# Three edits to the start of the mixture-of-experts stages of a fused transformer kernel: where expert 2's weights are asked for, where the first tokens are gathered, and 24 transposes of the identity on TensorE

## The chip, the cores and the metric

The kernel is one program on one core of a Trainium2 chip. Its time is that of one execution on the device, in microseconds (us). The engines named below are TensorE (PE, with its weight loads as PEld), VectorE (DVE), ScalarE (ACT), GpSimd (POOL) and SyncE (SP). SP does no arithmetic here, it issues the large DMA transfers. POOL issues the indirect ones, which gather or scatter rows by an index.

## The reference

Two blocks run one after the other on 512 tokens of width 1024 in float32. The first has two layers with a mixture of experts each; the second is a hybrid attention layer with a dense MLP. The change lies in the two mixtures, 768 tokens in layer 0 (512 and 256 context tokens) and 512 in layer 1:

```
lg = t @ wr_g + br_g ; g = argmax(lg)                       # 4 groups
le = (t @ wr_e + br_e) of group g                           # 8 experts in a group
top_v, top_i = top_k(le, 2)
weights = softmax(lg)[g] * softmax(top_v)
for each of the 32 experts, over the tokens that chose it:
    hidden = silu(x @ w_gate[e]) * (x @ w_up[e])            # 1024 -> 512
    y = hidden @ w_down[e]                                  # 512 -> 1024
out[token] += weight * y
```

The weights of one expert are three matrices of 1024 x 512 float32, 2 MB (2,097,152 bytes) each. All 32 experts are read in both layers, whatever the tokens chose.

## The kernel before

The program is a chain of phases. Each phase has its own tiles and semaphores and one block of code for each engine; between two phases all five engines meet at a barrier (line 127 in the profile), so a phase begins when the slowest engine has left the one before. The barrier is gathered by POOL. A layer's phases around the change are:

- `project_out` (out0, out1): the attention's output projection, residual, second norm and the router's logits, tile by tile of 128 tokens. SP asks for the projection's weights, the vectors, and then, in `load_expert(sp, e, ring, 0, 0)`, for all three matrices of expert 0. After that it stores each normalised tile `h` to DRAM (line 1160); `h` has two buffers, so the norm of tile i waits until the store of tile i-2 has landed (line 1291 is the instruction behind that wait).
- `route`: on DVE and PE, from the logits to a table `r["index"]` that lists, for each expert, 64 token slots. Each token row is two halves of 512 numbers, so a block of 64 tokens is a tile of 128 x 512. SP asks for experts 1 and 2, six transfers of 2 MB.
- `experts` (moe0, moe1): 32 blocks, one per expert. The weights lie in a ring of three slots; expert i lies in slot i % 3. SP's `refill` asks for the gate matrix of expert i+3 as soon as PE has done the gate products of expert i (semaphore `gated`), then for up (`upped`), then for down (`downed`). POOL gathers the tokens of block i+2 once PE has transposed those of block i, and scatters the results.

In block i PE does 32 gate products (line 1823; the profile counts each float32 matmul of this kind twice), 32 up products, the transposes of the tokens of block i+1 (line 1807), two transposes of the hidden values, and 16 down products (line 1869). Before block 0 it waits for `x_in[0]`, the first gather, and transposes it (`turn_x(0)`).

At the start of `experts` DVE clears the two token tiles `xg` and the last expert's tile (line 2055, `cleared`), since a slot without a token is not written by the gather. POOL copies one column of the index (line 1729), waits for `cleared` and issues the gather (line 1734); it does so for blocks 0 and 1, and then goes on as PE frees tiles. DVE then computes the tokens' weights and the count of extra blocks (for experts with over 64 tokens), which no engine needs in block 0.

The ring's slots are allotted from the right side of SBUF: slot 0 before `project_out`, the gate and up parts of slot 2 and all others after it (`add_first_slot`, `add_other_slots`).

## Time and profile before

| | |
|---|---|
| three runs | 2841.88, 2844.44, 2845.53 us; median 2844.44 |
| profiled execution | 2844.95 us, span 2843.1 us |
| PE busy | 2463.8 us (87%) |
| DVE, ACT, POOL busy | 1004.4, 552.0, 166.1 us |
| DMA | 599.29 MB moved; 425 GB/s in most slices of both expert stages |
| layer 0: first weight issue in routing, first refill | 658.33, 691.82 us |
| layer 1: first weight issue in routing, first refill | 1518.60, 1548.69 us |

The page divides the span of 2843.1 us into 40 slices of 71 us. Slices 11 to 16 and 22 to 28 move 415 to 426 GB/s: those are the two expert stages. A timeline row reads: start in us, duration of the merged piece, engine, line, operation, output<-input, count, and in brackets how long the engine had been idle and what ended that. Windows rows give, for a stretch, the busy time of each engine with the number of its instructions, TensorE's granted clock as a share of full speed (1.00 is 2.4 GHz, 0.50 is 1.2 GHz), the busy share of the DMA engines, and the rate.

### The profile page before, as it was taken

What the parts mean: (1) busy time and instruction counts of PE and PEld (TensorE: products, weight loads), DVE (VectorE), ACT (ScalarE), POOL (GpSimd) and SP (SyncE); (2) the same over time, 40 slices, a digit from 0 to 9 for tenths busy, and PEclk for the clock granted to TensorE, in tenths of its full rate; (3) what the DMA queues carried; (4) which work ended last, traced back from release to release, by engine and by line L of the source; (5) the groups of instructions that cost most, each with busy time, mean ns of one, the idle gap of its engine ahead of it and who ended that gap; (6) DMA issues with size and microseconds to landing.
All of it is one profiled execution on the core that took longest, in us unless ns stands there. A gap on an engine that the chain in (4) does not pass through costs nothing. (4 is left out here: it accounts for less than half of the span.)

```text
span 2843.1 us, 30780 instructions
## 1 busy us (share of the span) xinstructions
PE 2463.8 (87%) x12293; PEld 1297.5 (46%) x12293; DVE 1004.4 (35%) x2156; ACT 552.0 (19%) x1229; POOL 166.1 (6%) x270
## 2 busy tenths in 40 slices
PE   7999898795997777797986998788697789999999
PEld 4444366443553333344743553434343654444444
DVE  3211177665322222465734322222365452110000
ACT  3000077311000000114711100000122541000000
POOL 0000000001121111000001121111000000000000
PEclk9999899896999999898997999999898899999999
DMA  8555400507999999711056999999700140212110
GB/s 279 203 193 178 166 15 1 210 30 298 424 425 425 426 425 426 282 45 34 2 195 276 423 424 425 425 425 424 281 16 1 51 168 25 89 59 89 59 59 30
DMA packets 112474, 599.29 MB, mean 211 GB/s; under 512 B 22796, under 2 KB 33332, under 8 KB 82632
## 3 DMA queue, kind: packets, MB, share of 16 engines
q1 hardware_dynamic: 101768, 576.26, 50.6%
q0 software_dynamic: 10560, 21.01, 1.9%
q8 instruction: 101, 1.65, 0.2%
q14 instruction: 45, 0.37, 0.0%
HBM read 580.35 MB, written 30.49 MB: 215 GB/s over the span
## 5 line engine op out<-in xcount | busy, mean ns | idle before, releaser
L1823 PE MATMUL moe_gate<-moe_wg,moe_xg_t 128*64 128x256 f32 x1984 | 244.4, 398 | 50.1 <-DMA moe_wg<-in_moe_w_gate 48.6
L1869 PE MATMUL moe_down<-moe_wd,moe_hid_t 128*64 128x512 f32 x1024 | 235.5, 601 | 47.3 <-DMA moe_wd<-in_moe_w_down 34.1
L1823 PE MATMUL moe_up<-moe_wu,moe_xg_t 128*64 128x256 f32 x1984 | 239.3, 392 | 42.9 <-DMA moe_wu<-in_moe_w_up 42.9
L490 PE MATMUL qkv_acc<-qkv_w,a_buffer 128*128 128x512 f32 x512 | 225.7, 594 | 0.3 <-PE qkv_mod_acc L379 0.3
L3125 PE MATMUL mlp_acc<-m_h,mlp_w 128*128 128x512 f32 x512 | 223.3, 597 | 2.9 <-PE mlp_acc L3125 1.8
L1823 PEld LDWEIGHTS moe_gate<-moe_wg,moe_xg_t 128*64 128x64 f32 x1984 | 149.1, 138 | 162.7 <-DMA moe_wg<-in_moe_w_gate 82.0
L3142 PE MATMUL mlp_acc<-mlp_w,mlp_u_t 128*128 128x512 f32 x512 | 220.0, 592 | 0.3 <-PE mlp_acc L3125 0.3
L1823 PEld LDWEIGHTS moe_up<-moe_wu,moe_xg_t 128*64 128x64 f32 x1984 | 145.7, 135 | 132.3 <-DMA moe_wu<-in_moe_w_up 61.9
L3125 PEld LDWEIGHTS mlp_acc<-m_h,mlp_w 128*128 128x128 f32 x512 | 97.3, 191 | 128.5 <-issue 128.5
L3142 PEld LDWEIGHTS mlp_acc<-mlp_w,mlp_u_t 128*128 128x128 f32 x512 | 97.2, 190 | 123.1 <-issue 122.8
L2052 DVE COPY moe_y<-moe_down 128x512 f32<-128x512 f32 x62 | 42.9, 692 | 311.6 <-PE moe_down L1869 311.6
L1343 PE MATMUL out_acc<-out_w,out_o_t 128*128 128x512 f32 x320 | 149.9, 629 | 2.8 <-ACT out_o_t L1186 2.8
L1869 PEld LDWEIGHTS moe_down<-moe_wd,moe_hid_t 128*64 128x64 f32 x1024 | 73.5, 137 | 165.1 <-issue 123.7
L490 PEld LDWEIGHTS qkv_acc<-qkv_w,a_buffer 128*128 128x128 f32 x512 | 94.8, 190 | 113.9 <-issue 108.5
L1916 ACT ACTIVATE moe_sig<-moe_gate 128x256 f32<-128x256 f32 x64 | 24.6, 384 | 550.9 <-PE moe_gate L1823 550.9
L2039 DVE TENSOR_SCALAR moe_sig<-moe_sig 128x256 f32<-128x256 f32 x62 | 18.4, 297 | 271.7 <-ACT moe_sig L1916 271.7
L2041 DVE RECIPROCAL moe_sig<-moe_sig 128x256 f32<-128x256 f32 x62 | 108.7, 1753 | 2.1
L1758 POOL DMA_INDIRECT moe_results<-moe_y,moe_y_idx x62 | 64.3, 1038 | 712.3 <-DVE moe_y L2052 712.3
L1343 PEld LDWEIGHTS out_acc<-out_w,out_o_t 128*128 128x128 f32 x320 | 63.8, 202 | 82.3 <-issue 77.8
L1909 ACT COPY moe_xg_t<-moe_x_tp 128x512 f32<-128x512 f32 x64 | 37.5, 586 | 318.3 <-PE moe_x_tp L1807 318.3
L3162 DVE TENSOR_TENSOR mlp_u_t<-mlp_u_t 128x512 f32<-128x512 f32 x32 | 22.2, 692 | 207.4 <-ACT mlp_u_t L3156 207.4
L745 PE MATMUL dif_score<-a_k,a_q 64*128 64x256 f32 (+1 forms) x320 | 65.9, 525 | 23.5 <-ACT dif_prob L849 19.9
(441 smaller groups left out, 3015.8 us busy)
## 6 DMA issues: line engine op xcount, KB each, us to landing
moe_wg<-in_moe_w_gate SPq DMA_DIRECT2D x64, 2048.0 KB, 42.6
moe_wu<-in_moe_w_up SPq DMA_DIRECT2D x64, 2048.0 KB, 42.6
moe_wd<-in_moe_w_down SPq DMA_DIRECT2D x64, 2048.0 KB, 42.7
qkv_mod_w<-in_mod_w SPq DMA_DIRECT2D x42, 1024.0 KB, 4.9
mlp_w<-in_w_up SPq DMA_DIRECT2D x8, 2048.0 KB, 12.7
mlp_w<-in_w_down SPq DMA_DIRECT2D x8, 2048.0 KB, 7.9
qkv_w<-in_a_w_qkv SPq DMA_DIRECT2D x12, 1024.0 KB, 9.6
moe_results<-dif_zeros SPq DMA_DIRECT2D x12, 512.0 KB, 5.2
```

Source lines behind the costliest of these rows:

```text
L490: mm = nc.tensor.matmul(acc[i % 4][:], h_t[:, k, t * P:(t + 1) * P], w[:, c % w_ring, k, :], start=(k == 0), stop=(k == KD - 1))
L745: mm = nc.tensor.matmul(unit(g, m)[:, n0:n0 + w], q_t[rows, h, t * P:(t + 1) * P], k_t[rows, h, n0:n0 + w], start=True, stop=True)
L1343: mm = nc.tensor.matmul(acc[j % 3][:], lhs(k), w[:, c, k, :], start=(k == 0), stop=(k == KD - 1))
L1758: nc.gpsimd.indirect_dma_start(result_halves, bass.IndirectOffsetOnAxis(ap=y_idx[b][:], axis=0), y[b][:], None, bounds_check=last_result, ...
L1823: mm = nc.tensor.matmul(acc[b][halves[f], 0:HF], x_t[:, k, c, :], w[:, c, k, :].rearrange("p (q f j) -> p f q j", f=2, j=2)[:, f], start=( ...
L1869: mm = nc.tensor.matmul(down[b][halves[c], :], hid_t[:, k, h, :], wd[z][:, 2 * h + k, c * NCHUNK:(c + 1) * NCHUNK], start=(k, h) == (0, 0) ...
L1909: nc.scalar.copy(xg_t[b][:].rearrange("p k c n -> p k (c n)"), x_tp[:]).then_inc(s["read_x"], 1)
L1916: nc.scalar.activation(sig[:], gate[b][:, 0:HF], ACT.Exp, scale=-1.0).then_inc(s["expd"], 1)
L2041: nc.vector.reciprocal(sig[:], sig[:]).then_inc(s["step"], 1)
L2052: nc.vector.tensor_copy(y[b][:], down[b][:]).then_inc(s["y_done"], 1)
L3125: mm = nc.tensor.matmul(acc[i % 8][:], wj[:, k, q * P:(q + 1) * P], h_t[:, k, :], start=(k == 0), stop=(k == KD - 1))
L3142: mm = nc.tensor.matmul(acc[2 * t + c][:], u_t[:, f, t * P:(t + 1) * P], wj[:, q, c * NCHUNK:(c + 1) * NCHUNK], start=(f == 0), stop=(f == ...
```

## The change

- `project_out` asks for the gate and up matrices of expert 2 right behind expert 0's, if slot 2 already has its tiles. That is so in layer 1 alone, where the new `add_second_slot` allots them before the phase. Layer 0 asks as before.
- `route` then asks, in layer 1, for expert 1 and the down matrix of expert 2: four transfers of 2 MB, not six.
- `route` has a part for POOL: it clears the three token tiles (DVE's clearing in `experts` is gone), waits for the index (`indexed`), copies its first two columns and issues the gathers of blocks 0 and 1. The token tiles, their index tiles and the semaphores `x_in` move from the `experts` phase into the ring's record. This is so in both layers.
- In `experts`, PE does 24 transposes of the identity into an accumulator that nothing reads before block 1 overwrites it, ahead of its wait for the first gather. This is so in both layers.

```diff
@@ project_out, SP @@
             if ring is not None:
                 load_expert(sp, e, ring, 0, 0)
+                if 2 in ring["wg"]:
+                    load_gate(sp, e, ring["layer"], ring, 2, 2)
+                    load_up(sp, e, ring["layer"], ring, 2, 2)
@@ route @@
         def _(sp):
-            for b in range(1, RING):
-                load_expert(sp, e, ring, b, b)
+            load_expert(sp, e, ring, 1, 1)
+            if second_begun:
+                load_down(sp, e, layer, ring, 2, 2)
+            else:
+                load_expert(sp, e, ring, 2, 2)
+
+        @block.gpsimd
+        def _(pool):
+            for x in (*ring["xg"], ring["y"]):
+                nc.gpsimd.memset(x[:], 0.0).then_inc(s["cleared"], 1)
+            pool.wait_ge(s["indexed"], 1)
+            for b in range(2):
+                nc.gpsimd.tensor_copy(ring["x_idx"][b][:], r["index"][:, 0, b:b + 1]).then_inc(
+                    s["idx_done"], 1)
+            pool.wait_ge(s["cleared"], 3)
+            for b in range(2):
+                gather_tokens(nc, e, ring, b, lambda: pool.wait_ge(s["idx_done"], 2))
...
-            v.tensor_scalar(r["index"][:, :, 0:NE], slots[:], half[:], None, ALU.add)
+            v.tensor_scalar(r["index"][:, :, 0:NE], slots[:], half[:], None, ALU.add).then_inc(
+                s["indexed"], 1)
@@ the ring @@
+WARM = 24
+def add_second_slot(nc, ring):
+    for name in ("wg", "wu"):
+        add_part(nc, ring, "second", name, 2)
+def gather_tokens(nc, e, ring, b, idx_done):
+    rows = e["h_dram"].rearrange("r (h d) -> (r h) d", h=2)
+    idx_done()
+    nc.gpsimd.indirect_dma_start(
+        ring["xg"][b][:], None, rows, bass.IndirectOffsetOnAxis(ap=ring["x_idx"][b][:], axis=0),
+        bounds_check=rows.shape[0] - 1, oob_is_err=False).then_inc(ring["x_in"][b], 16)
@@ experts, POOL, PE and DVE @@
-            for b in range(2):
-                gather(b, b, b + 1)
...
+            for _ in range(WARM):
+                nc.tensor.transpose(down[1][:, 0:P], e["ident"][:], e["ident"][:])
             pe.wait_ge(x_in[0], 16)
             turn_x(0)
...
-            for x in (*xg, xg_l):
-                v.memset(x[:], 0.0).then_inc(s["cleared"], 1)
             token_weights()
@@ layer_1 @@
         add_first_slot(nc, ring)
+        add_second_slot(nc, ring)
...
-        route(nc, e, 1, stream, logits, r, ring)
+        route(nc, e, 1, stream, logits, r, ring, True)
```

How the instructions stand. On SP, in layer 1 from the projection's end into routing, before:

```order
L1572 DMA moe_wg<-in_moe_w_gate 128x4096
L1579 DMA moe_wu<-in_moe_w_up 128x4096
L1586 DMA moe_wd<-in_moe_w_down 128x4096
L1160 DMA moe_tokens<-out_h 128x1024 x4
L127 UNCONDITIONAL_BRANCH
L1410 UNCONDITIONAL_BRANCH
L1572 DMA moe_wg<-in_moe_w_gate 128x4096
L1579 DMA moe_wu<-in_moe_w_up 128x4096
L1586 DMA moe_wd<-in_moe_w_down 128x4096
L1572 DMA moe_wg<-in_moe_w_gate 128x4096
L1579 DMA moe_wu<-in_moe_w_up 128x4096
L1586 DMA moe_wd<-in_moe_w_down 128x4096
```

and after:

```order
L1610 DMA moe_wg<-in_moe_w_gate 128x4096
L1617 DMA moe_wu<-in_moe_w_up 128x4096
L1624 DMA moe_wd<-in_moe_w_down 128x4096
L1610 DMA moe_wg<-in_moe_w_gate 128x4096
L1617 DMA moe_wu<-in_moe_w_up 128x4096
L1163 DMA moe_tokens<-out_h 128x1024 x4
L127 UNCONDITIONAL_BRANCH
L1414 UNCONDITIONAL_BRANCH
L1610 DMA moe_wg<-in_moe_w_gate 128x4096
L1617 DMA moe_wu<-in_moe_w_up 128x4096
L1624 DMA moe_wd<-in_moe_w_down 128x4096 x2
```

The gate and up transfers of expert 2 now stand ahead of the four stores of `h`, and four weight transfers are left behind them.

On POOL, around the start of layer 0's experts, before (`route0_...` and `moe0_...` are semaphores of those phases, `barrier_...gather` is the barrier between two phases):

```order
L127 UNCONDITIONAL_BRANCH
L132 ISA [waits barrier_Pool_Activation_PE_DVE_SP_gather] x3
L1722 UNCONDITIONAL_BRANCH
L1729 COPY moe_x_idx<-r_index 128x1
L1734 DMA moe_xg<-moe_tokens,moe_x_idx 128x512 [waits moe0_idx_done,moe0_cleared]
L1729 COPY moe_x_idx<-r_index 128x1
L1734 DMA moe_xg<-moe_tokens,moe_x_idx 128x512 [waits moe0_idx_done,moe0_cleared]
L1729 COPY moe_x_idx<-r_index 128x1 [waits moe0_turned_x]
```

and after:

```order
L132 ISA [waits barrier_Pool_Activation_PE_DVE_SP_gather] x2
L1422 UNCONDITIONAL_BRANCH
L1425 MEMSET moe_xg 128x512 x2
L1425 MEMSET moe_last_y 128x512
L1428 COPY moe_x_idx<-r_index 128x1 [waits route0_indexed]
L1428 COPY moe_x_idx<-r_index 128x1
L1586 DMA moe_xg<-moe_tokens,moe_x_idx 128x512 [waits route0_idx_done,route0_cleared]
L1586 DMA moe_xg<-moe_tokens,moe_x_idx 128x512 [waits route0_idx_done]
L127 UNCONDITIONAL_BRANCH
L132 ISA [waits barrier_Pool_Activation_PE_DVE_SP_gather]
L1758 UNCONDITIONAL_BRANCH
L1765 COPY moe_x_idx<-r_index 128x1 [waits moe0_turned_x]
```

The clearing, two index copies and two gathers now stand ahead of the barrier that ends routing; behind it POOL begins with the gather for block 2.

On PE, from the last routing products of layer 0 into block 0, before:

```order
L1429 MATMUL route_slots<-route_what,route_lane 64x64 [waits route0_lane_done]
L1429 MATMUL route_slots<-route_what,route_lane 64x64 x11
L127 UNCONDITIONAL_BRANCH
L1802 UNCONDITIONAL_BRANCH [waits barrier_Pool_Activation_PE_DVE_SP_release]
L1807 MATMUL moe_x_tp<-ident_sb,moe_xg 128x128 [waits moe0_x_in0]
L1807 MATMUL moe_x_tp<-ident_sb,moe_xg 128x128 x3
L1823 MATMUL moe_gate<-moe_wg,moe_xg_t 64x256 [waits moe0_read_x,moe0_g_in0]
L1823 MATMUL moe_gate<-moe_wg,moe_xg_t 64x256 x15
L1823 MATMUL moe_up<-moe_wu,moe_xg_t 64x256 [waits moe0_u_in0]
L1823 MATMUL moe_up<-moe_wu,moe_xg_t 64x256 x15
```

and after:

```order
L1448 MATMUL route_slots<-route_what,route_lane 64x64 x11
L127 UNCONDITIONAL_BRANCH
L1834 UNCONDITIONAL_BRANCH [waits barrier_Pool_Activation_PE_DVE_SP_release]
L1907 MATMUL moe_down<-ident_sb 128x128 x24
L1839 MATMUL moe_x_tp<-ident_sb,moe_xg 128x128 [waits moe0_x_in0]
L1839 MATMUL moe_x_tp<-ident_sb,moe_xg 128x128 x3
L1855 MATMUL moe_gate<-moe_wg,moe_xg_t 64x256 [waits moe0_read_x,moe0_g_in0]
L1855 MATMUL moe_gate<-moe_wg,moe_xg_t 64x256 x15
L1855 MATMUL moe_up<-moe_wu,moe_xg_t 64x256 [waits moe0_u_in0]
```

Between the barrier's release and the wait for the first gather (`moe0_x_in0`) there are 24 transposes of the identity.

## Rows read from the trace of the kernel before

**Rows 1.** The page's list of DMA issues: count, size of each, us to landing.

```profile
moe_wg<-in_moe_w_gate SPq DMA_DIRECT2D x64, 2048.0 KB, 42.6
```

**Rows 2.** Windows, middle of layer 1's expert stage: busy us by engine, clock, DMA share, GB/s.

```profile
1700.00:1720.00 20.00, 16.29 (x118) 8.28 (x118) 3.69 (x6) 1.65 (x4) 4.95 (x8) 1.00 1.01 426
```

**Rows 3.** PE in order of time, ends of both expert stages: start, us, [idle before <-releaser].

```profile
1144.53 3.65 PE L1869 MATMUL moe_down<-moe_wd,moe_hid_t 128*64 128x512 f32 x16 [0.59 <-DMA moe_wd<-in_moe_w_down]
...
1990.35 3.65 PE L1869 MATMUL moe_down<-moe_wd,moe_hid_t 128*64 128x512 f32 x16 [0.63 <-DMA moe_wd<-in_moe_w_down]
1996.80 5.45 PE L1823 MATMUL moe_gate<-moe_wg,moe_xg_t_l 128*64 128x256 f32 x32 [2.80 <-DMA moe_wg<-in_moe_w_gate]
```

**Rows 4.** SP's DMA issues in order of time, routing of layer 1 and after.

```profile
1518.60 0.33 SPq L1572 DMA_DIRECT2D moe_wg<-in_moe_w_gate  x1
...
1521.24 0.45 SPq L1586 DMA_DIRECT2D moe_wd<-in_moe_w_down  x1
1548.69 0.33 SPq L1572 DMA_DIRECT2D moe_wg<-in_moe_w_gate  x1
```

**Rows 5.** Windows, layer 1, from the first issue of the routing stage to the first refill.

```profile
1518.60:1525.00 6.40, 0.72 (x2) 0.50 (x2) 5.49 (x25) 1.28 (x1) 0.00 (x0) 0.50 0.86 317
1525.00:1548.50 23.50, 10.16 (x73) 6.79 (x74) 9.24 (x42) 0.90 (x3) 5.11 (x9) 0.52 1.01 427
```

**Rows 6.** PE in order of time, first block of layer 1.

```profile
1540.61 1.11 PE L1807 MATMUL moe_x_tp<-ident_sb,moe_xg 128*128 128x128 f32 x4 [11.05 <-DMA moe_xg<-moe_tokens,moe_x_idx]
1542.49 6.17 PE L1823 MATMUL moe_gate<-moe_wg,moe_xg_t 128*64 128x256 f32 x32 [0.77 <-ACT moe_xg_t L1909]
1548.48 3.80 PE L1823 MATMUL moe_up<-moe_wu,moe_xg_t 128*64 128x256 f32 x32
```

**Rows 7.** DVE and POOL in order of time, between routing and experts, layer 1.

```profile
1529.60 0.28 DVE L1487 TENSOR_SCALAR r_index<-route_slots,half_sb 128x64 int32<-128x64 f32 x1 [1.56 <-PE route_slots L1429]
...
1530.40 0.19 POOL L1729 COPY moe_x_idx<-r_index 128x1 int32<-128x1 int32 x1 [356.10 <-POOLq L127]
1532.49 1.06 POOL L1734 DMA_INDIRECT moe_xg<-moe_tokens,moe_x_idx  x1 [1.91 <-DVE moe_last_y L2055]
...
1534.61 1.04 POOL L1734 DMA_INDIRECT moe_xg<-moe_tokens,moe_x_idx  x1 [0.85 <-POOL moe_x_idx L1729]
```

**Rows 8.** Windows, layer 0, around the first refill.

```profile
690.00:695.00 5.00, 5.00 (x43) 3.30 (x42) 2.47 (x3) 0.38 (x1) 0.00 (x0) 0.93 0.74 241
```

**Rows 9.** POOL, PE and SP in order of time, same stretch of layer 0.

```profile
674.81 1.20 POOL L1734 DMA_INDIRECT moe_xg<-moe_tokens,moe_x_idx  x1 [1.65 <-DVE moe_last_y L2055]
...
683.62 1.12 PE L1807 MATMUL moe_x_tp<-ident_sb,moe_xg 128*128 128x128 f32 x4 [11.49 <-DMA moe_xg<-moe_tokens,moe_x_idx]
685.50 6.29 PE L1823 MATMUL moe_gate<-moe_wg,moe_xg_t 128*64 128x256 f32 x32 [0.77 <-ACT moe_xg_t L1909]
...
691.82 0.33 SPq L1572 DMA_DIRECT2D moe_wg<-in_moe_w_gate  x1
```

**Rows 10.** Windows in the first gate products of layer 1.

```profile
1547.50:1548.00 0.50, 0.50 (x6) 0.30 (x4) 0.00 (x0) 0.00 (x0) 0.00 (x0) 1.00 0.84 356
```

**Rows 11.** PE in order of time, transposes of the second block's attention.

```profile
2202.03 5.42 PE L2882 MATMUL turn_tp<-ident_sb,c_hh 128*128 128x128 f32 x32 [2.64 <-DVE turn_dk L2849]
```

**Rows 12.** Windows in those transposes.

```profile
2203.00:2206.00 3.00, 3.00 (x16) 2.79 (x15) 1.53 (x5) 2.06 (x5) 0.00 (x0) 0.50 0.37 62
2207.00:2208.00 1.00, 1.00 (x12) 1.00 (x10) 0.96 (x2) 1.00 (x3) 0.00 (x0) 1.00 0.07 16
```

**Rows 13.** POOL in order of time, the clearing of a tile of zeros.

```profile
340.37 0.95 POOL L733 MEMSET dif_zeros<- 128x1024 f32 x1 [338.69 <-POOLq L127]
```

**Rows 14.** SP and DVE in order of time, layer 1's output projection.

```profile
1465.45 0.33 SPq L1160 DMA_DIRECT2D moe_tokens<-out_h  x1
...
1490.53 2.00 DVE L1291 SCALAR_TENSOR_TENSOR out_h<-res,out_n_rstd,out_mul 128x1024 f32<-128x1024 f32 x1 [0.31 <-DVE out_n_rstd L162]
```

**Rows 15.** Windows, layer 1's output projection.

```profile
1465.00:1470.00 5.00, 3.70 (x25) 3.32 (x26) 3.71 (x6) 2.13 (x3) 0.00 (x0) 0.90 0.58 243
```

More of the change, by code:

```diff
@@ L1384, in max_extra, with route @@
     return 4 * nt
-def route(nc, e, layer, tiles, logits, r, ring):
+def route(nc, e, layer, tiles, logits, r, ring, second_begun):
     nt = len(tiles)
@@ L1405, in route @@
         where, slots = ph.ps("where", [P, nt + 1, NE]), ph.ps("slots", [P, 2, NE])
-        names = "zeroed hot_done what_done where_done lane_done slots_done gexp_in wexp_in step"
+        names = ("zeroed hot_done what_done where_done lane_done slots_done gexp_in wexp_in cleared indexed "
+                 "idx_done step")
         s = {x: ph.sem(x) for x in names.split()}
@@ L1499, in weight_ring @@
                 next_in=[one(f"next_in{c}") for c in range(5)], vec_in=[one(f"vec_in{x}") for x in range(2)],
-                last_out=one("last_out"))
+                last_out=one("last_out"), x_in=[one(f"x_in{b}") for b in range(2)])
 def add_part(nc, ring, scope, name, b):
@@ L1512, in add_first_slot @@
         add_part(nc, ring, "first", name, 0)
+def add_second_slot(nc, ring):
+    for name in ("wg", "wu"):
+        add_part(nc, ring, "second", name, 2)
 def add_other_slots(nc, ring):
-    add_part(nc, ring, "second", "wg", 2)
-    add_part(nc, ring, "second", "wu", 2)
+    if 2 not in ring["wg"]:
+        add_second_slot(nc, ring)
     for name, shape, dt in (("y", [P, NCHUNK], F32), ("hit", [P, P], F32), ("share", [P, 1], F32),
@@ L1525, in add_other_slots @@
         add_part(nc, ring, "scope", name, 1)
+    for name, shape, dt in (("xg", [P, D // 2], F32), ("x_idx", [P, 1], I32)):
+        ring[name] = [ring["scope"].enter_context(
+            nc.sbuf_tensor(f"moe{ring['layer']}_{name}{b}", shape, dt, side="right")) for b in range(2)]
 def flat(part):
@@ L1644, in experts @@
         wg, wu, wd = ring["wg"], ring["wu"], ring["wd"]
-        xg = [ph.sb(f"xg{b}", [P, D // 2]) for b in range(2)]
+        xg, x_idx, x_in = ring["xg"], ring["x_idx"], ring["x_in"]
         xg_t = [ph.sb(f"xg_t{b}", [P, 4, 2, TB]) for b in range(2)]
-        x_idx = [ph.sb(f"x_idx{b}", [P, 1], I32) for b in range(2)]
         y_idx = [ph.sb(f"y_idx{b}", [P, 1], I32) for b in range(2)]
@@ L1677, in experts @@
         part = [gate[0][:], up[0][:]]
-        names = ("y_free cleared idx_done turned_x read_x gated upped expd hid_done indexed landed "
+        names = ("y_free idx_done turned_x read_x gated upped expd hid_done indexed landed "
                  "turned_h read_h downed y_done step x_step x_tables_done x_slots_done x_read x_ready "
@@ L1681, in experts @@
         s = {x: ph.sem(x) for x in names.split()}
-        x_in = [nc.alloc_semaphore(f"moe{layer}_x_in{b}") for b in range(2)]
         x_in_l = nc.alloc_semaphore(f"moe{layer}_x_in_l")
@@ L1731, in gather @@
                 pool.wait_ge(s["idx_done"], count)
-                pool.wait_ge(s["cleared"], 2)
                 pool.sem_inc(s["indexed"], 1)
@@ L1743, in gather_last @@
                 pool.wait_ge(s["idx_l_done"], 1)
-                pool.wait_ge(s["cleared"], 3)
                 pool.sem_inc(s["indexed"], 1)
@@ L1769, in _ @@
                     pool.wait_ge(s["x_ready"], 1)
-                gather(b, i + 2 if i + 2 < last else i + 3, 2 * i + 3)
+                gather(b, i + 2 if i + 2 < last else i + 3, 2 * i + 1)
                 if i == 0:
                     gather_last()
-                scatter(b, i, i, 2 * i + 4)
+                scatter(b, i, i, 2 * i + 2)
                 if i >= 1:
@@ L1783, in two_extra @@
                     pool.wait_ge(s["turned_x"], i + 1)
-                    gather(b, i + 3, 2 * i + 3)
-                    scatter(b, i + 1, i, 2 * i + 4)
+                    gather(b, i + 3, 2 * i + 1)
+                    scatter(b, i + 1, i, 2 * i + 2)
                     pool.wait_ge(y_out[1 - b], 16 * (NE // 2 + i2))
@@ L2139, in layer_0 @@
     with ring["scope"]:
-        route(nc, e, 0, tiles, logits, r, ring)
+        route(nc, e, 0, tiles, logits, r, ring, False)
         experts(nc, e, 0, tiles, r, ring, TC, enter_1_loads)
@@ L2380, in layer_1 @@
         add_first_slot(nc, ring)
+        add_second_slot(nc, ring)
         project_out(nc, e, "out1", o, stream, None, None, 1.0, e["b_w_o"][0], mod_part(e, 1, 2),
```

## The prediction

> **What bounds the kernel now.** I read the page's slices first: both expert stages move some 425 GB/s from end to end. Then the windows of one of them: PE is busy 16.3 of 20 us at full clock while the DMA engines are busy all the time, at 426 GB/s [rows 2]. Then PE's order of time where each stage ends: the last full block's down products still wait for their weights [rows 3]. So each stage is one stream of 2 MB transfers (2.097 MB each [rows 1], 4.93 us at 425 GB/s), and PE follows it. The layer ends when the stream ends plus a fixed tail: an instant by which the whole stream comes earlier is an instant off the total, and an engine made faster in mid-stream is worth nothing.
>
> Next, where the stream has a hole. Its head start in routing is six transfers. The seventh is asked for when PE has done the first gate products: at 1548.69 in layer 1 [rows 4], right after those products (1542.49 + 6.17 = 1548.66 [rows 6]). In layer 1 the rate up to then is 427 GB/s [rows 5]: no hole. In layer 0 the same request, at 691.82 [rows 9], comes late, and the window around it shows 241 GB/s [rows 8]: (1 - 241/425) x 5 = 2.2 us of stream lost. A stream that starts from nothing loses too: from the first issue at 1518.60 to 1525 it made 317 GB/s [rows 5], (1 - 317/425) x 6.4 = 1.6 us, which I take as the price of a start.
>
> **Part 1, expert 2's gate and up in layer 1's projection.** Two transfers leave the routing stream: 2 x 4.93 = 9.9 us. But four transfers and the first two gathers (128 x 512 float32, 0.26 MB each) are 8.91 MB, 21.0 us, so the stream runs dry at 1518.6 + 1.6 + 21.0 = 1541.2, before the first refill can be asked for. So the gain is decided by when PE finishes gate products 0, that is by parts 2 and 3.
>
> What the two transfers cost where they now stand: the queue goes quiet at about 1465 + 5 x 243/425 = 1467.9 [rows 15]; 9.9 us more makes it 1477.7, while the projection's matmuls have their weights already. The first store of h is issued at 1465.45, and the norm that needs its buffer again starts at 1490.53 [rows 14]. Cover 12.8 us, cost nothing; if the cover is gone, each us late is a us lost (last rival).
>
> **Part 2, the gathers.** The index is ready at 1529.60 + 0.28 = 1529.88 [rows 7]. Before, POOL passed the barrier, copied at 1530.40 and then waited for DVE's clearing until 1532.49. Now: two copies of 0.2, 0.85 from a copy to the gather behind it, so the first gather at about 1531.2, 1.3 us sooner. Before it took 1540.61 - 1532.49 = 8.1 us until PE had the tokens [rows 6, 7], and the stream is as full in this stretch as before, so they land at 1539.3. The third gather and the last expert's come behind block 0's token transposes as before; POOL has nothing queued behind them that is urgent.
>
> What is added: the clearing is now on POOL, at the head of routing. 1024 columns took 0.95 us [rows 13], so three tiles of 512 cost 1.4 us, done 10 us before the index. It lies beside DVE's short routing operations. The trace has no POOL clearing beside busy DVE; bounds are 0 and, if the two engines exclude one another for all of it, 1.4 us. I take 0.4, near the lower end, since an engine writing its own tile is the nearest row. DVE loses its 1.5 us of clearing, which were on the path only through the gather. And the barrier: routing now ends for all engines only after POOL's second gather, at 1531.2 + 1.06 + 1.04 + 0.44 = 1533.7, not 1530.4. DVE's weights and counts begin 3.3 us later less 1.5; the first value that block 0 needs from DVE is behind the gate products, which ended at 1548.66 before [rows 6], so that is hidden.
>
> **Part 3, the 24 transposes.** They begin at 1533.7. Four transposes at half clock took 1.11 us [rows 6], so at most 24 x 0.28 = 6.7 us; 32 in a row, partly at full clock, took 5.42 [rows 11], so at least 24 x 0.17 = 4.1. Middle 5.4: they end at 1539.1, just before the tokens at 1539.3 (bounds 1537.8 and 1540.4). So T0, the start of token transposes, is 1539.4.
>
> What they are to give is the clock. Before, block 0's gate products ran at a mean of 0.52 [rows 5]; the clock rose to 1.00 at 1547.5 [rows 10], with PE at work since 1540.61. They took 6.17 us where the up products took 3.80 [rows 6]; the token transposes took 1.11, against 0.66 by the same ratio. In the attention of the second block PE did nothing but transposes from 2202.03 on [rows 11], at 0.50 at first and at 1.00 by 2207 [rows 12]. So transposes alone do raise the clock here. The Trainium skill says the opposite in "TensorE: Matmul & The Clock Gate", Part 4: a transpose does not count as PE activity and full clock "doesn't engage" for it. By that rule the 24 give nothing; by the row they give all. I follow the row, and the other way is a rival.
>
> At full clock the gate products end at T0 + 0.66 + 0.77 + 3.80 = T0 + 5.2 = 1544.6, or 1545.1 if the token transposes are still slow. I take 1544.9, 3.8 us sooner than before.
>
> **Sum.** Layer 1: the stream is dry from 1541.2 until 1544.9 + 1.6 = 1546.5, 5.3 us. In that hole the two next gathers move 0.52 MB, 1.2 us of what the stream would carry later. Gain 9.9 - 5.3 + 1.2 = 5.8. Layer 0: nothing leaves its stream, but the refill is asked for 3.8 us sooner, at 688.0; the stream ends at 691.82 + 1.6 - 2.2 = 691.2, later than 688.0 + 1.6, so the hole closes: gain 2.2, and 1.6 us in hand. Less 0.4 for the clearing: 7.6 us. From the profiled execution, 2844.95 (1.85 over its span, which stays), that is 2837.4. The median of the three runs stands 0.5 lower, which makes 2836.9; I say 2837.1.
>
> **The rivals.** A change of 0.2%, 5.7 us, is about what can be told from none.
>
> The clock does not rise (the page's rule, or the clock falls again while PE waits for the tokens). For it: the clock was at 0.50 through routing's small products. Against: rows 11 and 12. Gate products then end at T0 + 8.05 = 1547.5. Layer 1: 5.8 - 2.6 = 3.2. Layer 0: the request comes at 690.6, 1.0 past need, gain 1.2. Less 0.4: 4.0 us, 2841.0.
>
> The wait turned into another: barrier and transposes are later than the tokens. If the second gather needs the 0.85 pause too and each transpose takes 0.28, they run from 1534.5 to 1541.2, T0 1.8 later: layer 1 gives 4.0, layer 0 2.0, sum 5.6, 2839.3. For it: the barrier is gathered by POOL, the order shows the transposes ahead of the wait, and PE can't leave them. Against: it needs both upper ends.
>
> Better than forecast: the tokens land sooner, or the clock is up earlier than I put it, T0 + 5.2 with T0 at 1538. 1.7 us more, 2835.4. The gather's 8.1 us speaks against it.
>
> Slower: the stores of h behind the extra weights. At 1465.45 there are 1.04 + 4.19 = 5.2 MB ahead of the first store. Every us past 1490.5 stops the norm of tile 2, PE's transposes and the router behind it. The gain of 7.6 is eaten when the store lands at 1498.1, that is at 160 GB/s; over 0.2% slower needs 1503.8, 136 GB/s, and gives 2851. For it: the queue is one and in order. Against: the same stretch moved 243 GB/s in a window of which it was busy 0.58 [rows 15], so over 400 while busy.
>
> **How the numbers follow.** Forecast 0.60 (0.55 of it beyond 0.2%), better 0.08, no clock 0.13, later transposes 0.15 (half of it beyond 0.2%), slower 0.04. Faster 0.55 + 0.08 + 0.07 = 0.70, same 0.05 + 0.13 + 0.08 = 0.26, slower 0.04. The range takes in the better case with 0.8 us of spread below it, and above it the case without clock and the whole price of the clearing in layer 1: 2834.6 to 2842.0.
>
> **What would show it.** In the changed profile: five weight issues in the projection of layer 1 and the same norm start after the first store; a gather some 1.3 us after the index, in routing; PE's 24 transposes from 3.3 us after where it used to arrive, and a granted clock of 1.00 before the gate products, which take 3.8 us in both layers; first refill 3.8 us sooner against the first issue in both; in layer 0 no window under 415 GB/s around it, in layer 1 one with a hole of some 5 us before it; then blocks at the old pace to the end. The forecast is wrong if the clock is at 0.50 in the gate products, if the tokens or the transposes come later than 1540 by that clock, if routing's DVE chain is longer by over a us, or if the stream at 425 GB/s turns out not to carry its earlier start to the stage's end.

## The result

| | us |
|---|---|
| changed kernel, 22 runs | median 2852.19 (2847.47 to 2870.25) |
| kernel before, 22 runs beside them | median 2843.55 |
| ratio, 95% interval | 1.0027 [1.0015, 1.0039] |
| changed kernel, profiled execution | 2852.25, span 2850.4 |

The change makes the kernel 0.27% slower, 8.6 us by the medians. The forecast was 2837.1 (2834.6 to 2842.0), with a chance of 0.04 for slower: the measured time is 10.2 us above the range, and the sign is wrong. Two of the profiled executions read below, of the gathers alone (2860.20 us) and of 64 transposes alone (2854.86), are 11 to 12 us over their medians; the surplus lies behind layer 1's expert stage (860.3 and 861.5 us from there to the end, 849.1 before), so their stages can be read.

### The profile page after: what moved, and what is told of

It reads as the page before. It is cut to its first block and busy times, and to the rows that moved or that the text cites. A ratio compares the mean times of both kernels' runs of the same rounds, so it can differ in the third digit from the quotient of the medians.

```text
span 2850.4 us, 30876 instructions
## 1 busy us (share of the span) xinstructions
PE 2461.1 (86%) x12341; PEld 1301.5 (46%) x12341; DVE 1001.6 (35%) x2150; ACT 551.5 (19%) x1229; POOL 168.2 (6%) x276
```

## The profile after

I read it in the order of the prediction's steps. First POOL, in order of time, from the start of routing in layer 1; it answers to [rows 7] and [rows 13].

```profile
1521.73 0.98 POOL L1425 MEMSET moe_xg<- 128x512 f32 x2 [343.53 <-POOLq L127]
1522.66 0.53 POOL L1425 MEMSET moe_last_y<- 128x512 f32 x1
1533.24 0.30 POOL L1428 COPY moe_x_idx<-r_index 128x1 int32<-128x1 int32 x2 [10.06 <-DVE r_index L1506]
1534.43 1.07 POOL L1586 DMA_INDIRECT moe_xg<-moe_tokens,moe_x_idx  x1 [0.89 <-POOL moe_x_idx L1428]
1535.81 1.02 POOL L1586 DMA_INDIRECT moe_xg<-moe_tokens,moe_x_idx  x1 [0.31 <-issue]
```

POOL does what was forecast, when it was forecast: the first gather 1.26 us after the index (1532.89 + 0.28 = 1533.17), the second 1.38 behind the first, its last instruction of routing over at 1536.83. By the prediction's term the next phase should begin 0.44 us later, at 1537.3. PE and DVE in order of time, the same layer, against [rows 6]:

```profile
1545.50 5.35 PE L1907 MATMUL moe_down<-ident_sb 128*128 128x128 f32 x24 [12.65 <-PEq L127]
1550.65 0.85 PE L1839 MATMUL moe_x_tp<-ident_sb,moe_xg 128*128 128x128 f32 x4
1552.27 3.85 PE L1855 MATMUL moe_gate<-moe_wg,moe_xg_t 128*64 128x256 f32 x32 [0.77 <-ACT moe_xg_t L1943]
```

```profile
1532.89 0.28 DVE L1506 TENSOR_SCALAR r_index<-route_slots,half_sb 128x64 int32<-128x64 f32 x1 [1.56 <-PE route_slots L1448]
1545.50 0.17 DVE L1985 TENSOR_REDUCE moe_chosen<-r_tg 128x4 f32<-128x16 f32 x1 [12.32 <-PEq L127]
```

PE had been idle for 12.65 us and DVE for 12.32, both at line 127, the barrier. They leave it at 1545.50, 8.7 us after POOL's last instruction. What was in flight in those 8.7 us is in the list of DMA issues for the two gathers of routing (last number: median us from issue to landing):

```profile
moe_xg<-moe_tokens,moe_x_idx POOLq DMA_INDIRECT x2, 8.9
```

The 8.9 is the middle of the two: the first took 8.6 us, the second 9.3. So the second landed at 1535.81 + 9.3 = 1545.1, 0.4 us ahead of the barrier's end. In layer 0 it was issued at 676.12, took 10.5 us and landed at 686.6, again 0.4 us ahead of PE's first work at 687.01. The windows say the same from the DMA side, and stand against [rows 5] (us, busy by engine, clock, DMA share, GB/s):

```profile
1525.00:1540.00 15.00, 3.75 (x36) 2.82 (x36) 5.78 (x22) 0.31 (x2) 2.39 (x4) 0.50 1.02 434
1540.00:1543.00 3.00, 0.00 (x0) 0.00 (x0) 0.00 (x0) 0.00 (x0) 0.00 (x0) 0.50 0.95 399
1543.00:1544.50 1.50, 0.00 (x0) 0.00 (x0) 0.00 (x0) 0.00 (x0) 0.00 (x0) 0.50 0.17 60
1544.50:1545.50 1.00, 0.00 (x0) 0.03 (x1) 0.00 (x0) 0.00 (x0) 0.00 (x0) 0.50 0.00 0
...
1548.50:1550.00 1.50, 1.50 (x9) 1.50 (x8) 1.26 (x8) 0.00 (x0) 0.00 (x0) 0.50 0.00 0
1550.00:1552.00 2.00, 1.50 (x9) 1.26 (x7) 1.14 (x7) 0.47 (x1) 0.18 (x1) 0.71 0.00 0
1552.00:1556.00 4.00, 3.73 (x34) 2.81 (x36) 0.00 (x0) 0.12 (x1) 2.43 (x4) 1.00 0.08 22
```

The stream thins out at about 1543, hardly any bytes move after 1544.5, and only then does an engine move. Here the weights and the gathers end nearly together, so this trace alone does not say which of them the barrier waits for. The transposes then run with every DMA engine silent: they are on the path, all 5.2 us of them. They do what they were put there for, the clock is at 1.00 in the gate products, which take 3.85 us and not 6.17. The first refill answers to [rows 4]; above it the weight issues of routing:

```profile
1521.47 0.33 SPq L1610 DMA_DIRECT2D moe_wg<-in_moe_w_gate  x1
...
1522.33 1.24 SPq L1624 DMA_DIRECT2D moe_wd<-in_moe_w_down  x2
1556.14 0.33 SPq L1610 DMA_DIRECT2D moe_wg<-in_moe_w_gate  x1
```

Layer 0, PE and SP in order of time, against [rows 9]:

```profile
687.01 4.74 PE L1907 MATMUL moe_down<-ident_sb 128*128 128x128 f32 x24 [14.04 <-PEq L127]
691.59 0.60 PE L1839 MATMUL moe_x_tp<-ident_sb,moe_xg 128*128 128x128 f32 x4
692.96 3.84 PE L1855 MATMUL moe_gate<-moe_wg,moe_xg_t 128*64 128x256 f32 x32 [0.77 <-ACT moe_xg_t L1943]
...
696.83 0.33 SPq L1610 DMA_DIRECT2D moe_wg<-in_moe_w_gate  x1
```

When the index is ready varies by several us from one execution to the next, from work far upstream. So I count from the index in each layer ("+" below), and take as the stage's length the time from there to SP's first request for the layer after (`moe_wd<-mod_scratch`), which comes when the ring comes free at the end. These two rows are of the kernel before:

```profile
1148.22 0.33 SPq L1716 DMA_DIRECT2D moe_wd<-mod_scratch  x1
1994.04 0.33 SPq L1716 DMA_DIRECT2D moe_wd<-mod_scratch  x1
```

and these of the changed one:

```profile
1153.87 0.33 SPq L1752 DMA_DIRECT2D moe_wd<-mod_scratch  x1
2002.34 0.33 SPq L1752 DMA_DIRECT2D moe_wd<-mod_scratch  x1
```

| layer 0 / layer 1, us | before | after |
|---|---|---|
| index ready | 672.44 / 1529.88 | 673.29 / 1533.17 |
| PE begins the tokens' transposes | +11.18 / +10.73 | +18.30 / +17.48 |
| first refill | +19.38 / +18.81 | +23.54 / +22.97 |
| stage's length | 475.78 / 464.16 | 480.58 / 469.17 |

The start is 7.12 and 6.75 us late, the warm clock gives 2.96 and 2.59 back, the refill is 4.16 us late in both layers, and the stages are 4.80 and 5.01 us longer: 9.8 together. The profiled spans differ by 7.3; the rest is 0.85 more before layer 0's index, and 2.4 and 1.0 less between the layers and behind them.

## The experiments

Theory 1: POOL does not join the barrier until the data of its own gathers have landed. Its rivals: the transposes or the moved weights cost the time, or the barrier waits for the stream of weights. Each run is compared with runs of the kernel before on its own chip.

**Gathers back in `experts`, all else as changed.**

```diff
 route, POOL:
-            (copies of the index, gathers of blocks 0 and 1)
 experts, POOL, at its start:
+            for b in range(2):
+                nc.gpsimd.tensor_copy(x_idx[b][:], r["index"][:, 0, b:b + 1]).then_inc(
+                    s["idx_0_done"], 1)
+                gather_tokens(nc, e, ring, b, lambda: pool.wait_ge(s["idx_0_done"], b + 1))
```

> The changed kernel with one thing undone: the first two gathers (and their index copies) are issued by POOL at the start of the expert stage again, not in routing; the clearing stays in routing, expert 2's early weights and the 24 transposes stay. Theory 1 (POOL cannot join the barrier at routing's end before the data of its own gathers have landed; in the changed kernel PE and DVE start 12.3 us after the index in layer 1 and 13.8 us in layer 0, 0.44 before): the expert stage starts within 0.6 us of the index, the transposes lie inside the wait for the tokens, gate products 0 run at full clock, and the first refill comes about 15.3 us after the index in layer 1 (18.8 before, 23.0 changed); time about 2837, some 7 below the kernel before and 15 below the changed one. Theory 2 (the loss is the extra weights in layer 1's projection or POOL's clearing beside DVE): no better than the changed kernel, 2850 or more. Theory 3 (the 24 transposes are the loss, not the gathers): they still end after the tokens, 2846 or more.

Measured: 2841.67, ratio 0.9996 [0.9981, 1.0011]. PE in order of time, layer 1:

```profile
1525.65 4.51 PE L1904 MATMUL moe_down<-ident_sb 128*128 128x128 f32 x24 [0.64 <-PEq L127]
1536.31 1.12 PE L1836 MATMUL moe_x_tp<-ident_sb,moe_xg 128*128 128x128 f32 x4 [6.15 <-DMA moe_xg<-moe_tokens,moe_x_idx]
1538.19 5.99 PE L1852 MATMUL moe_gate<-moe_wg,moe_xg_t 128*64 128x256 f32 x32 [0.77 <-ACT moe_xg_t L1940]
```

The stage begins 0.32 us after the index and the loss is gone, so it hangs on gathers issued ahead of the barrier, as theory 1 says. SP's weights do not hold the barrier: they moved at 433 GB/s ahead of it (1520.0 to 1525.3) and at 420 behind it (1526 to 1530). But the gain, expected at 2837, does not come either. With the barrier out of the way the transposes end 6.15 us before the tokens, and the gate products are slow again. Windows of layer 0, where the same is seen (clock is the third number from the right):

```profile
672.10:675.00 2.90, 2.88 (x24) 2.72 (x24) 2.44 (x14) 0.00 (x0) 1.58 (x3) 0.95 1.01 424
675.00:677.00 2.00, 0.06 (x1) 0.00 (x0) 1.69 (x10) 0.00 (x0) 1.03 (x1) 1.00 1.00 422
...
679.00:682.00 3.00, 0.00 (x0) 0.00 (x0) 0.00 (x0) 0.00 (x0) 0.00 (x0) 0.54 1.01 421
682.00:684.00 2.00, 1.14 (x6) 0.78 (x6) 0.00 (x0) 0.59 (x1) 0.18 (x1) 0.50 1.00 416
```

The clock was at 1.00 when the transposes ended and at 0.50 when the tokens came; it fell while PE waited.

**Each part alone.** The gathers alone are the changed kernel without transposes and without the moved weights:

```diff
-WARM = 24
+WARM = 0
 before project_out of layer 1:
-        add_second_slot(nc, ring)
-        route(nc, e, 1, stream, logits, r, ring, True)
+        route(nc, e, 1, stream, logits, r, ring, False)
```

The weights alone are the kernel before with the edits to `project_out`, `add_second_slot` and SP's part of `route`. The transposes alone are the kernel before with this, the output tile being the same:

```diff
+            for _ in range(24):
+                nc.tensor.transpose(down[1][:, 0:P], e["ident"][:], e["ident"][:])
             pe.wait_ge(x_in[0], 16)
```

> Clearing, copies and first two gathers in routing, as in the changed kernel, and nothing else of it: no transposes, expert 2 asked for in routing as before. Theory 1: PE starts on the tokens only when the second gather has landed, 12 to 14 us after the index; gate products at half clock, 6.2 us; first refill 2.6 us later against the index in layer 0 and 1.6 in layer 1. Layer 0's stream has a hole already and loses 2.6, layer 1's has 1.4 us in hand and loses 0.2: 2846 to 2847, 3 above before. If the barrier does not wait for the data: PE has the tokens 1.3 us sooner than before, 2842 to 2843.

> The kernel before with expert 2's gate and up asked for in layer 1's projection, nothing else. The stream of layer 1 runs dry 22.6 us after routing's first issue and the refill comes 30.1 after it as before, so the hole is 9.1 us with the start, less 1.2 for the gathers that move in it; gain 9.9 - 9.1 + 1.2 = 2.0: 2841 to 2842. If the extra transfers delay the stores of h (rival): the norm of tile 2 starts late and the time is 2846 or more.

> The kernel before with the 24 transposes of the identity ahead of the wait for the first gather, nothing else. They begin 0.5 us after the index and end some 5 us before the tokens. If the clock rises and is still up when the tokens come: gate products 0 take 3.8 us, the first refill 2.8 us sooner in both layers; layer 0 gains its hole of 2.2, layer 1 nothing since its stream has no hole: 2841. If transposes do not raise the clock, or it falls again in the 5 us of waiting: gate products at half clock again, no difference in time, 2843.5.

| | time | ratio | refill, layer 0 / 1 | gate products | stage's length |
|---|---|---|---|---|---|
| gathers alone | 2849.28 | 1.0020 [1.0004, 1.0036] | +20.81 / +21.53 | 5.44 / 6.44 | 477.07 / 466.26 |
| weights alone | 2843.02 | 1.0003 [0.9992, 1.0014] | +19.66 / +18.81 | 6.38 / 6.03 | 476.05 / 463.54 |
| transposes alone | 2843.58 | 1.0002 [0.9993, 1.0012] | +17.83 / +19.87 | 5.09 / 6.38 | 474.24 / 465.05 |

Moving the gathers is slower by itself: its interval lies above 1, and its stages are 1.3 and 2.1 us longer than before, where 2.6 and 0.2 were expected. This kernel also settles the last rival: its routing asks for six transfers of weights, and they are still moving when the barrier opens. PE and the window around it, layer 1:

```profile
1544.97 1.09 PE L1839 MATMUL moe_x_tp<-ident_sb,moe_xg 128*128 128x128 f32 x4 [13.52 <-PEq L127]
```

```profile
1544.00:1546.00 2.00, 1.03 (x4) 0.72 (x4) 0.86 (x6) 0.00 (x0) 0.00 (x0) 0.50 1.02 434
```

The second gather, issued at 1534.41, took 10.2 us and landed at 1544.6; 0.4 us later PE moves, with the weights at full rate.

The weights alone shorten layer 1's stage by 0.6 us, with the refill where it was. That is less than the 1.2 us by which layer 1's stage differs among the kernels that move neither weights nor gathers (464.16 to 465.33, each from one profiled execution), so no gain is shown, and of the 2.0 us expected at most a part can be there. The transposes alone end 7.0 and 7.7 us before the tokens and lose the clock; their 24 also took 3.5 us, less than the prediction's lower bound of 4.1.

**The changed kernel without the transposes.**

```diff
-WARM = 24
+WARM = 0
```

> The changed kernel without its 24 transposes; all else as changed. Theory 1 (the barrier at the end of routing waits for POOL's gathers, so PE comes 12 to 14 us after the index, with the tokens already landed): the transposes are path, 4.74 us in layer 0 and 5.35 us in layer 1, and buy 2.4 us of gate products each (6.2 to 3.84) and 0.3 to 0.5 us of the turning: the first refill comes 4.74 - 2.45 - 0.5 = 1.8 us sooner after the index than in the changed kernel in layer 0 (+21.7) and 2.2 us in layer 1 (+20.8); the time falls by about 4 us to 2848. Rival (the transposes still cover a wait, the loss is elsewhere): refill no sooner, gate products half clocked, time 2852 to 2857.

Measured: 2846.15, ratio 1.0004 [0.9987, 1.0022]. PE in layer 1:

```profile
1543.05 1.08 PE L1839 MATMUL moe_x_tp<-ident_sb,moe_xg 128*128 128x128 f32 x4 [12.41 <-PEq L127]
1544.90 5.42 PE L1855 MATMUL moe_gate<-moe_wg,moe_xg_t 128*64 128x256 f32 x32 [0.77 <-ACT moe_xg_t L1943]
```

The tokens are transposed as soon as the barrier opens, with no wait for data: they had landed. The refill is at +20.79 and +19.40, so counted from the index the 24 transposes cost 2.8 and 3.6 us net; by the medians they are 6 of the 8.6 (expected were 2848 and 4 us). The cost is somewhat more than the 1.8 and 2.2 expected, since part of the gate products (5.5 and 5.4 us, not 6.2) is at full clock without them.

**One gather in routing, the other in `experts`.** This and the next ask what the barrier waits for.

```diff
 route, POOL:
-            for b in range(2):
-                gather_tokens(nc, e, ring, b, lambda: pool.wait_ge(s["idx_done"], 2))
+            gather_tokens(nc, e, ring, 0, lambda: pool.wait_ge(s["idx_done"], 2))
 experts, POOL, at its start:
+            gather_tokens(nc, e, ring, 1, lambda: None)
```

> The changed kernel with only the first of the two gathers in the routing stage; POOL issues the second as its first work in the experts' stage. Theory 1a (the barrier waits for the data of every gather that POOL issued in the stage): the first work of PE and DVE in the experts' stage comes when the first gather has landed, 10 to 12.5 us after the index, 0 to 1.5 us sooner than in the changed kernel (12.33 and 13.72). Rival 1b (the barrier waits only for POOL's last instruction in the stage, and that last one was somehow long): the stage begins about 2.6 us after the index or less. The second block's products then wait for the later second gather; no time is forecast from this one look.

One run, 2841.72. POOL and PE, layer 1:

```profile
1528.33 1.07 POOL L1585 DMA_INDIRECT moe_xg<-moe_tokens,moe_x_idx  x1 [0.89 <-POOL moe_x_idx L1428]
...
1537.40 4.39 PE L1907 MATMUL moe_down<-ident_sb 128*128 128x128 f32 x24 [10.64 <-PEq L127]
...
1538.32 1.01 POOL L1585 DMA_INDIRECT moe_xg<-moe_tokens,moe_x_idx  x1 [8.92 <-issue]
```

The DMA list for the gather of routing:

```profile
moe_xg<-moe_tokens,moe_x_idx POOLq DMA_INDIRECT x1, 8.7
```

The one gather took 8.7 us to land, 1528.33 + 8.7 = 1537.0, and PE leaves the barrier at 1537.40. POOL itself did nothing from 1529.40 on. So it is not a long instruction, and not the number of gathers.

**The gathers land in a quiet machine.** SP asks for expert 1's and 2's remaining weights at the start of `experts`, not in routing.

```diff
 route, SP:
-            load_expert(sp, e, ring, 1, 1)
-            (expert 2, or its down matrix)
+            pass
 experts, SP, at its start:
+            load_expert(sp, e, ring, 1, 1)
+            load_down(sp, e, layer, ring, 2, 2) if layer else load_expert(sp, e, ring, 2, 2)
```

> The changed kernel, but the weights of experts 1 and 2 that the routing stage asks for are asked for by SP at the start of the experts' stage instead, so that in layer 1 (and in layer 0 once expert 0's are in) the two gathers land with no stream of weights beside them. Theory 1a (the barrier comes when the gathers' data have landed): with the engines of the queues free the data land sooner, some 3 to 5 us after their issue instead of 8.9, and PE and DVE start the stage 5 to 8 us after the index instead of 12.33 and 13.72. Rival 1c (the drain after an indirect DMA takes a fixed time, whatever the transfer does): the start stays at 12 to 14 us after the index. The whole is slower by far, since the weights come late: 2870 to 2900 us; its time is not what it is run for.

One run, 2868.31. POOL and PE in layer 1, and the DMA list for the two gathers:

```profile
1548.45 1.02 POOL L1582 DMA_INDIRECT moe_xg<-moe_tokens,moe_x_idx  x1 [0.31 <-issue]
...
1551.53 5.36 PE L1905 MATMUL moe_down<-ident_sb 128*128 128x128 f32 x24 [6.04 <-PEq L127]
```

```profile
moe_xg<-moe_tokens,moe_x_idx POOLq DMA_INDIRECT x2, 2.8
```

With nothing beside them the gathers land in 2.8 us (2.9 the first, 2.7 the second) and the barrier opens at 1551.53, 3.1 us after the second issue instead of 9.7. The wait follows the transfer, so a fixed price of the barrier is out. Five kernels issue gathers ahead of the barrier: the changed one, the gathers alone, no transposes, one gather, the quiet one. In their ten layers the last such gather took 2.7 to 10.5 us to land, and PE's first work came 0.36 to 0.46 us behind the landing in the nine for which the trace has it (all but layer 0 of the one gather).

It also prices the stream: a gather takes 2.8 us alone and 8.9 beside the weights. The two move less than their tiles hold, since a slot without a token is not read. This is the gathers' DMA queue in the changed kernel, 1533 to 1546 us (packets, MB, share of the engines):

```profile
q0 software_dynamic: 160, 0.21, 4.3%
```

The Trainium skill ("DMA: Bandwidth & Descriptors", section "Anatomy of one DMA — SWDGE (gpsimd) path") fits the time of such a DMA by about 2.0 us plus the bytes at 436 GB/s. For 0.10 MB that makes 2.2 us, an estimate; the quiet run is 0.6 us above it, the busy one 6.7 us.

**More transposes, so that PE works until the tokens land.** The first experiment's kernel with

```diff
-WARM = 24
+WARM = 64
```

then with 84, and with 64 once more.

> Gathers issued by POOL in the experts' stage as before the change (tile clearing left in routing), the extra weights as changed, and 64 transposes instead of 24, so that PE is busy up to about when the tokens land. In the variant with 24 the transposes ran 0.33 to 4.8 us after the index, the granted clock was 1.00 behind them and 0.54 by the time the turning of the tokens began (+10.3 and +10.98), and the gate products took 6.40 and 5.99 us. Theory (the clock fell because PE idled 5 to 7 us): 64 transposes at 0.17 us from a warm start last 10.5 to 11 us, to about +11; the gate products take 3.84 us and the turning 0.6 to 0.85 in place of 1.12, and the first refill comes at +16.0 to +16.8 instead of +18.6 and +18.9: 2.3 us sooner in each layer, time 2838 (2836 to 2840), ratio 0.9975 to 0.9990. Rival A (the streams are not behind the refill, so that a sooner refill buys nothing): the marks as said, time 2841 to 2843. Rival B (64 overrun the tokens by 1 to 2 us): turning at +12 to +13, refill at +17 to +18, time 2840 to 2842.

> As the variant with 64 transposes, with 84. The 64 took 7.79 and 7.74 us (0.12 us each), ended 1.5 and 2.1 us before the turning of the tokens (+9.63 and +10.20 after the index), and the gate products took 5.44 and 5.45 us, not 3.84; the first refill came at +16.52 and +17.10. Theory (PE's idle time before the tokens is what lets the clock fall): 84 last 10.2 us, to +10.6, so the turning begins at about +10.6, 0.4 to 1.0 us later than with 64, the gate products take 3.84 us and the first refill comes at +15.9 to +16.1 in both layers; time 2837 (2835 to 2840). Rival (the fall of the clock at the gate products comes from the waits around the turning, not from the 2 us before it): gate products again 5.4 us, refill at +17.0 to +17.6, time 2839 to 2841.

> The variant with gathers back in the experts' stage, extra weights and 64 transposes, once more, since its ratio of 0.9981 [0.9966, 0.9996] and the 0.9997 of the one with 84 have stages of the same length by their traces (473.45 and 473.28 us in layer 0 from the index to the first request for the layer's later weights, 462.92 and 462.78 in layer 1, against 475.78 and 464.16 before). Theory: both stages together are 3.5 us shorter than before, the clearing on POOL costs 0.4 to 0.7 in routing, so ratio 0.9985 to 0.9992, time 2839.5 to 2841. Rival (a true gain of 5 us): ratio 0.998 or less again.

| | time | ratio | transposes last | PE then idle | gate products | refill | stage's length |
|---|---|---|---|---|---|---|---|
| 64 | 2838.23 | 0.9981 [0.9966, 0.9996] | 7.79 / 7.74 | 1.5 / 2.1 | 5.44 / 5.45 | +16.52 / +17.10 | 473.45 / 462.92 |
| 84 | 2841.19 | 0.9997 [0.9977, 1.0017] | 10.23 / 11.42 | 0 / 0 | 3.84 / 3.85 | +15.63 / +16.83 | 473.28 / 462.78 |
| 64 again | 2838.85 | 0.9985 [0.9970, 1.0001] | 9.73 / 8.85 | 0 / 0.94 | 3.84 / 3.85 | +15.20 / +15.41 | 473.69 / 462.03 |

PE in layer 1, 64 again:

```profile
1526.48 8.85 PE L1904 MATMUL moe_down<-ident_sb 128*128 128x128 f32 x64 [0.65 <-PEq L127]
1536.27 0.66 PE L1836 MATMUL moe_x_tp<-ident_sb,moe_xg 128*128 128x128 f32 x4 [0.94 <-DMA moe_xg<-moe_tokens,moe_x_idx]
1537.70 3.85 PE L1852 MATMUL moe_gate<-moe_wg,moe_xg_t 128*64 128x256 f32 x32 [0.77 <-ACT moe_xg_t L1940]
```

The first 64 took 7.8 us where 10.5 to 11 were expected; PE then waited again, and the gate products were not the 3.84 us expected. With no wait, or 0.94 us of it, ahead of the tokens the gate products run at full clock. All three have stages 3.6 to 4.2 us shorter than before in sum. By the medians the version with 64 came out 5.3 and 5.6 us below the kernel before, once with an interval that excludes 1 and once with one that touches it. The second ratio, 0.9985, is what was expected of a gain of the size of the stages' (0.9985 to 0.9992), and not of a true gain of 5 us (0.998 or less). It is the best version found. That the 84 measured 2841.19, where 2837 was expected, with stages as short is not explained by the traces; its interval covers both.

**The kernel before with transposes alone, 84 and 64 of them** (`range(24)` above made `range(84)` and `range(64)`).

> The kernel before with nothing but 84 transposes of the identity on PE ahead of the first tokens; gathers, clearing and weights as before the change. Theory (the clock at the first gate products is all of what can be had, the extra weights in the projection give nothing because the first refill is asked for by PE's gate products): the turning at about +10.8 (layer 0) and +11.2 (layer 1) as before, gate products 3.84 us instead of 6.29 and 6.17, first refill at +16.5 and +16.9 instead of +19.38 and +18.81, and the stage as a whole 2 us shorter in each layer; time 2839 to 2840, ratio 0.998 to 0.999, within its interval of the variant with the extra weights. Rival (the extra weights give 2 us or more of their own once the refill comes sooner, since the stream is asked for earlier in layer 1): this one stays at 2841 to 2842 while the variant with them comes to 2837.

> The kernel before with 64 transposes alone, no weights moved. Theory: layer 0 gains what its hole held, 2 us, if the first refill comes at +17 or sooner after the index; layer 1 gains nothing, since without the extra weights its stream has no hole (with 84 transposes its refill came 2.2 us sooner and the stage was not shorter, 465.33 against 464.16 us): ratio 0.9990 to 1.0000, stage of layer 0 at 473.3 to 474, of layer 1 at 464 to 465.5 us. Rival (layer 1 gains with its refill too): stage of layer 1 at 462 to 463, ratio 0.9985 or less.

| | time | ratio | gate products | refill | stage's length |
|---|---|---|---|---|---|
| 84 | 2842.55 | 0.9999 [0.9982, 1.0016] | 6.64 / 3.85 | +20.73 / +16.63 | 476.99 / 465.33 |
| 64 | 2842.97 | 0.9992 [0.9982, 1.0001] | 6.42 / 3.85 | +19.38 / +16.19 | 475.56 / 465.18 |

In layer 1 the refill comes 2.2 and 2.6 us sooner than before and the stage is not shorter: without the moved weights there is no hole to close. About the same refill with them gives 462 to 463, so they are worth 2.3 to 3.3 us once the refill is early (those kernels also clear on POOL, which puts their first gather 0.7 us sooner), and 0.6 us, inside the spread of 1.2, while it is not. Neither the weights nor the transposes show a gain alone. In layer 0 the tokens came at +12.64 and +11.30 (before: +11.18) and PE idled 3.0 and 3.3 us after the transposes; the gate products were slow, the refill no sooner, and the expected 2 us could not be seen. That the layer 1 stages are 1 us over the 464.16 of the kernel before is left open.

## Why the prediction was wrong, step by step

- **The step that failed** is in part 2: "routing now ends for all engines only after POOL's second gather, at 1531.2 + 1.06 + 1.04 + 0.44 = 1533.7". It took the end of POOL's issuing for the time at which POOL can join. By that sum the barrier opens 3.8 us after the index; it opened at +12.33 and +13.72. The runs with one gather, with the gathers alone and with a quiet machine show what is missing: the landing of the last gather, 9.3 us after its issue in layer 1 and 10.5 in layer 0. The term of 0.44 itself was right, but it counts from that landing. The size of the wait was in the rows (8.1 us from gather to PE), applied to PE's wait for the tokens and not to the barrier.
- **Part 3** followed it down. Cover ("they run from 1533.7 to 1539.1, just before the tokens") became path, since a barrier that opens when the last tokens have landed leaves no wait to fill. Without the transposes the loss is 2.6 us by the medians, which its interval does not tell from none; with them it is 8.6.
- The transposes raise the clock: right. At 1545.5 to 1550 PE did nothing else, at 0.50, and it was at 1.00 from 1552, with nothing but transposes up to 1551.5. The rule weighed in the prediction ("TensorE: Matmul & The Clock Gate", Part 4, of the Trainium skill: full clock doesn't engage for transposes) does not hold for these float32 transposes.
- But 24 of them could at best fit a barrier that opens at +3.8, as the prediction had it, and no run has that barrier. Where the stage starts with the index, 24 are over 6 to 8 us before the tokens, and the clock is lost again. The rival named this ("the clock falls again while PE waits for the tokens"), at 0.13.
- **Part 1**: no delay of the stores of h, right. The first store was issued at 1468.88 and the norm of tile 2 began 24.2 us later, 25.1 before [rows 14], with no wait ahead of it:

```profile
1468.88 0.33 SPq L1163 DMA_DIRECT2D moe_tokens<-out_h  x1
...
1493.12 2.00 DVE L1294 SCALAR_TENSOR_TENSOR out_h<-res,out_n_rstd,out_mul 128x1024 f32<-128x1024 f32 x1
```

- The slower rival was thus the wrong mechanism on the right side. The rival "the wait turned into another" had the right place, barrier and transposes behind the tokens, but priced the barrier at 1534.5, 0.8 us more than the forecast; measured are 8.5 more in layer 1 and 9.9 in layer 0.
- **Clearing** 0.4 us, right for one layer: first issue to the end of the index is 11.28 us before and 11.70 after in layer 1, 0.34 more in layer 0. But the sum takes it off once, and it is paid in both. One DVE operation beside POOL's memset took 0.61 us where it took 0.17 before:

```profile
1519.74 0.17 DVE L1459 TENSOR_SCALAR route_away<-route_hot_g 128x16 f32<-128x16 f32 x1
...
1522.61 0.61 DVE L1478 TENSOR_SCALAR route_away<-route_hot_g 128x16 f32<-128x16 f32 x1
```

- **The sum** had layer 0 at 2.2 and layer 1 at 5.8 us. With the barrier free and the clock up (64 again: refill at +15.20 and +15.41, the forecast 15.0 in layer 1) layer 0 gives 2.1 and layer 1 2.1. So layer 0's term was right. Layer 1's was too large by 3.7. Its hole was reckoned with full tiles, 0.52 MB for two gathers and 8.91 with the four transfers. The queue moved 0.21 MB for the first two, 8.60 in all from the first issue at 1514.46 to 1537, so the stream ran dry 0.7 us sooner than reckoned. The two gathers behind them moved 0.24 MB, which is 0.6 us of the stream and not 1.2. Another 0.4 is the refill at +15.41. The other 2.0 were not traced; 1 us of them may be the spread of layer 1's stage. Start and end of that stream, layer 1:

```profile
1516.00:1526.00 10.00, 3.75 (x36) 2.81 (x36) 7.39 (x28) 0.31 (x2) 0.17 (x1) 0.50 0.96 406
...
1530.00:1535.00 5.00, 5.00 (x48) 5.00 (x47) 2.29 (x12) 0.00 (x0) 1.04 (x1) 1.00 1.02 431
1535.00:1537.00 2.00, 0.99 (x8) 0.51 (x5) 0.00 (x0) 0.03 (x1) 0.00 (x0) 1.00 0.56 226
1537.00:1541.00 4.00, 3.30 (x30) 2.50 (x32) 0.00 (x0) 0.55 (x1) 2.41 (x4) 1.00 0.10 26
```

- The times of two rivals, 2841.0 and 2851, are counted from the profiled execution, and the forecast from 0.3 us below it; nothing above hangs on it.

## What to carry to other kernels

Before moving an indirect DMA of POOL ahead of a barrier, price the barrier at the landing of that DMA, beside whatever else is in flight; to start a transfer early across a phase boundary, it must come from a queue for whose data the boundary does not wait (SP's loads of weights cross it freely here), or the boundary must go. Work put on an engine to fill a wait is free only while there is a wait behind it: look at what opens the point where it starts, and whether the data will have landed by then. And work that is to keep the clock up should last until the real work starts: in these runs up to 0.94 us between them did no harm, 1.5 us did in one case of two. Count a gather by the rows that it reads, not by its tile.

## What the runs showed of the hardware that was not expected

- This program's barrier does not open while a gather that POOL issued in the phase is under way. From the index to PE's first work: 13.72 and 12.33 us (layer 0, layer 1) with two gathers beside the weight stream, 9.86 and 10.33 with one, 6.57 and 5.72 with two while no weights were asked for in routing, 0.33 and 0.32 with none. From the last gather's landing to PE's first work it is 0.36 to 0.46 us. SP's transfers do not hold the barrier: with the gathers alone moved, the stream stood at 434 GB/s from 1544 to 1546, and the barrier opened at 1544.97.
- The granted clock fell from 1.00 to 0.50 within 7 us of PE's waiting. These are the first gate products where the stage started with the index, by how long PE had waited between transposes and tokens: 3.84 or 3.85 us in the five cases with 0 to 0.94 us of waiting and in one with 1.5; 5.44 and 5.45 with 1.5 and 2.1; 6.42 and 6.64 with 3.3 and 3.0; 5.09 to 6.40 with 6 to 8. The two cases with 1.5 us on either side, and the 5.09 behind 7.0 us of waiting, show that the wait is not all that counts; what else does was not tried.
- The same 24 transposes took from 2.94 us (mean granted clock 0.95) to 5.36 (0.50 for most of it).
